# A decoder layer on one core: attention and mLSTM parts get step tables of their own, DVE makes the last weight remainders

## The reference, cut to what matters

```python
z = x @ w_in
q_a, k_a, v_a, q_idx, k_idx, w_idx, q_m, k_m, v_m, o_m, i_m, f_m = jnp.split(z, split_points, axis=-1)
y_a = _dsa_attention(...)          # score = sum_h w[t,h] relu(q_idx.k_idx); top 128 causal keys; softmax with ALiBi
qk_m = silu(causal_depthwise_conv(concat[q_m, k_m], conv_w, conv_b))
y_m = _mlstm(q_m, k_m, v_m, i_m + b_igate, f_m + b_fgate, o_m, gn_w)   # 4 heads of 128, head normalisation at the end
mix = concat([y_a, y_m]) @ w_out
x = layer_norm(alpha * x + mix);  x = layer_norm(alpha * x + hier_moe(x))
x = x + sigmoid(x @ ple_gate_w) * (p @ ple_proj_w)
```

## Time and profile before

| what | us |
|---|---|
| median of 3 runs (750.93 to 752.8) | 751.52 |
| profiled execution, its own time | 750.55 |
| its span, first to last instruction | 748.8 |
| PE busy (matmuls) | 653.2 |
| DVE busy | 338.9 |
| ACT busy | 178.6 |
| POOL busy | 208.8 |

### The profile page before, as it was taken

How to read it: one execution, slowest core, us unless ns; L and a number is a source line. 1 busy time by engine, 2 the same in 40 slices (tenths; PEclk the granted TensorE clock), 3 DMA queues, 4 the chain that set the end, 5 groups by cost and what they waited for, 6 DMA issues and landing times.

```text
span 748.8 us, 10018 instructions
## 1 busy us (share of the span) xinstructions
PE 653.2 (87%) x3782; PEld 456.1 (61%) x3782; DVE 338.9 (45%) x791; ACT 178.6 (24%) x344; POOL 208.8 (28%) x177
## 2 busy tenths in 40 slices
PE   4999649999999999899644999999999988866997
PEld 3768537787787788678532555555555544422776
DVE  3389995284265254654863211111112211148932
ACT  5264112422423313710120111111111111132230
POOL 7215400540451130450202233333333331112300
PEclk9959779999999999999875999999999999989899
DMA  6402300130130050029287688999999999957002
GB/s 242 170 1 85 140 1 0 57 141 1 56 113 1 1 224 1 2 95 397 104 347 311 232 325 296 405 416 415 413 414 415 415 416 415 414 196 285 1 35 78
DMA packets 30438, 151.21 MB, mean 202 GB/s; under 512 B 7308, under 2 KB 7564, under 8 KB 16432
## 3 DMA queue, kind: packets, MB, share of 16 engines
q1 hardware_dynamic: 23984, 142.08, 48.0%
q0 software_dynamic: 6400, 8.42, 3.1%
HBM read 148.36 MB, written 14.68 MB: 218 GB/s over the span
## 4 chain that ended last, share of the span: by engine, by line
PE 56%; DVE 12%; DMA 6%; SPq 5%; issue 3%; ACT 1%; POOL 0%; DVEq 0%; POOLq 0%; ACTq 0%
PE bank L1798 15%; PE bank L1813 8%; PE bank L1507 7%; PE bank L1509 7%; PE bank L1508 7%; SPq L422 5%; DMA raw<-in_w_exp_dram 4%; PE bank L1587 3%; PE bank L1788 2%; PE bank L1596 2%; PE bank L1608 2%; DVE res L1482 1%; DVE res L1207 1%; DVE res L1092 1%; PE bank L1637 1%
## 5 line engine op out<-in xcount | busy, mean ns | idle before, releaser
L1437 DVE COPY rows_x<-bank 128x128 f32<-128x128 f32 x40 | 11.7, 292 | 194.9 <-issue 101.3
L1507 PE MATMUL bank<-w_hi,a_hi 128*128 128x384 f32 (+1 forms) x256 | 95.7, 374 | 3.2 <-DVE w_lo L1491 1.7
L1508 PE MATMUL bank<-w_lo,a_hi 128*128 128x384 f32 (+1 forms) x256 | 94.0, 367 | 0.0
L1509 PE MATMUL bank<-w_hi,a_lo 128*128 128x384 f32 (+1 forms) x256 | 93.9, 367 | 0.0
L633 POOL DMA_INDIRECT pair_dram<-rows_x,row_put x40 | 40.5, 1013 | 166.7 <-ACT rows_x L872 166.7
L1507 PE MATMUL bank<-a_hi,w_hi 128*128 128x512 f32 (+1 forms) x176 | 70.9, 403 | 11.3 <-POOL w_lo L543 9.9
L543 POOL TENSOR_TENSOR w_lo<-raw,w_hi 128x1024 fp32r<-128x1024 f32 x19 | 45.2, 2386 | 120.8 <-ACT w_hi L680 120.7
L1798 PE MATMUL bank<-raw,rows_x 128*64 128x256 f32 x544 | 65.4, 392 | 7.0 <-DMA raw<-in_w_exp_dram 5.4
L1508 PE MATMUL bank<-a_lo,w_hi 128*128 128x512 f32 (+1 forms) x176 | 68.9, 391 | 0.0
L1509 PE MATMUL bank<-a_hi,w_lo 128*128 128x512 f32 (+1 forms) x176 | 68.7, 390 | 0.0
L1798 PEld LDWEIGHTS bank<-raw,rows_x 128*64 128x64 f32 x544 | 40.2, 141 | 36.3 <-issue 14.6
(11 more groups left out here) (238 smaller groups left out, 1016.6 us busy)
## 6 DMA issues: line engine op xcount, KB each, us to landing
raw<-in_w_exp_dram SPq DMA_DIRECT2D x42, 1024.0 KB
slots<-in_w_exp_dram SPq DMA_DIRECT2D x36, 1024.0 KB
rows_x<-in_w_exp_dram SPq DMA_DIRECT2D x12, 1024.0 KB
raw<-in_w_in_dram SPq DMA_DIRECT2D x19, 512.0 KB, 3.8
raw<-in_w_wide_dram SPq DMA_DIRECT2D x4, 1536.0 KB, 6.6
y<-in_w_exp_dram SPq DMA_DIRECT2D x6, 1024.0 KB
raw<-in_w_out_dram SPq DMA_DIRECT2D x4, 1024.0 KB, 7.8
raw<-pair_dram SPq DMA_DIRECT2D x4, 1024.0 KB, 8.7
```

The source lines that it names most:

```text
L1507: t_.matmul(o, lh, rh, start=first, stop=False)
L1508: t_.matmul(o, lh, rl, start=False, stop=False)
L1509: return t_.matmul(o, ll, rh, start=False, stop=last)
```

## The change

- Each part gets a list of step numbers, one per head. `ATTEND` gives the step of the first attention sub-step (12, 18, 24, 30), and the six follow in the six steps from there. `HEAD_QK`, `HEAD_NUM`, `BROADCAST`, `DECAY_EXP`, `CONV`, `TANH`, `CONV_END`, `HEAD_VAR` and `HEAD_OUT` do the same for the parts of an mLSTM head.
- DVE makes the remainders of pieces 11 to 18 (`split`) and of the wide weights of groups 2 and 3 (`split_wide`); POOL keeps the rest.
- `lstm_out` is in two parts, `lstm_variance` and `lstm_out`, and `convolve` too: the taps, and `convolve_end` with the product. For this the tanh has a buffer of its own for q and for k (parts of `weight` and `dist` that are free then).
- On ACT, `gates_last` of step 1 stands behind `round_piece` and `round_wide` of that step.

```diff
+        ATTEND = [12, 18, 24, 30]
+        BROADCAST, DECAY_EXP = [5, 15, 20, 28], [8, 16, 21, 29]
+        CONV, TANH, CONV_END = [[None, None], [13, 14], [19, 22], [27, 28]], [[9, 10], [15, 15], [22, 23], [28, 29]], [9, 16, 24, 30]
+        HEAD_QK, HEAD_NUM, HEAD_VAR, HEAD_OUT = [12, 17, 24, 30], [14, 19, 26, 32], [15, 20, 26, None], [16, 21, 29, None]
+        POOL_PIECES, POOL_WIDE = 11, 2
...
@@ POOL
-                if i is not None and i + RING < NPIECE:
+                if i is not None and i + RING < POOL_PIECES:
                     split(i + RING)
-                if grp is not None and j == 1:
+                if grp is not None and j == 1 and grp < POOL_WIDE:
                     split_wide(grp)
...
@@ ACT
-                if 2 * h + c >= 1:
-                    act.wait_ge(s_conv, 2 * h + c)
-                a.activation(tanh_c, conv[:, c, :], ACT.Tanh, scale=0.5).then_inc(s_ctanh, 1)
+                if h:
+                    act.wait_ge(s_conv, 2 * h)
+                    act.wait_ge(s_mdist, 6)
+                a.activation(tanh_of(h, c), conv[:, c, :], ACT.Tanh, scale=0.5).then_inc(s_ctanh, 1)
...
-                if n == step_no(0, 1):
-                    gates_last()
                 i = piece_at(n)
                 if i is not None and i + RING < NPIECE:
                     round_piece(i + RING)
                 if grp is not None and j == 1:
                     round_wide(grp)
+                if n == step_no(0, 1):
+                    gates_last()
...
@@ DVE
+            def split(i):
+                dve.wait_ge(s_wlo, i)
+                dve.wait_ge(s_whi, i + 1)
+                r = i % RAWS
+                v.tensor_tensor(ring(w_lo, i), raw[:, r * PW:(r + 1) * PW], ring(w_hi, i).bitcast(F32),
+                                ALU.subtract).then_inc(s_wlo, 1)
...
             def work(g, j):
+                now = STEPS * g + j
+                for h in range(HM):
+                    if CONV_END[h] == now:
+                        convolve_end(h, 0)
+                        convolve_end(h, 1)
+                    if 0 <= now - HEAD_QK[h] < 2:
+                        lstm_weight(h, 2 * (now - HEAD_QK[h]))
+                        lstm_weight(h, 2 * (now - HEAD_QK[h]) + 1)
+                for h in range(NG):
+                    if 0 <= now - ATTEND[h] < 6:
+                        attention(h, now - ATTEND[h])
+                if g < NG and j < TALL and POOL_PIECES <= SMALL + TALL * g + j + RING < NPIECE:
+                    split(SMALL + TALL * g + j + RING)
+                if POOL_WIDE <= g < NG and j == 1:
+                    split_wide(g)
+                for h in range(HM):
+                    if h and BROADCAST[h] == now:
+                        lstm_add(h)
+                    for c in range(2):
+                        if CONV[h][c] == now:
+                            convolve(h, c)
+                    if HEAD_VAR[h] == now:
+                        lstm_variance(h)
+                    if HEAD_OUT[h] == now:
+                        lstm_out(h)
```

More of the change, by code:

```diff
@@ L140, in hybrid_layer, with tanh_of @@
         conv = res[:, 2560:3584].rearrange("p (a t) -> p a t", a=2)
-        tanh_c = res[:, 3584:4096]
+        tanh_q = res[:, 3584:4096]
+        def tanh_of(h, c):
+            return (dist[:, :] if h else weight[:, 0:512]) if c else tanh_q
         at = [0]
@@ L574, in _ @@
                     strike_future()
[L575 removed]
+                if i is not None and i + RING < POOL_PIECES:
                     split(i + RING)
[L577 removed]
+                if grp is not None and j == 1 and grp < POOL_WIDE:
                     split_wide(grp)
[L579 to L582, removed]
+                if grp is not None:
+                    for h in range(HM):
+                        if DECAY_EXP[h] == n - SMALL:
+                            mask_decay(h)
+                        if HEAD_VAR[h] == n - SMALL:
+                            power(h)
             def split_out(q):
@@ L773, in work @@
             def work(g, j):
[L775 to L785, removed]
+                now = STEPS * g + j
+                for h in range(HM):
+                    if HEAD_NUM[h] == now:
+                        lstm_hidden(h)
+                for h in range(NG):
+                    if 0 <= now - ATTEND[h] < 6:
+                        attention(h, now - ATTEND[h])
+                for h in range(HM):
+                    if DECAY_EXP[h] == now:
+                        lstm_exp(h)
+                    for c in range(2):
+                        if TANH[h][c] == now:
+                            conv_tanh(h, c)
             def round_x(c):
@@ L1096, in convolve, with step_post, settle_post, lstm_variance @@
                     dve.wait_ge(s_mqk, 4 * h)
-                v.scalar_tensor_tensor(out=qk_m[:, c, :], in0=tanh_c, scalar=1.0, in1=conv[:, c, :], op0=ALU.add,
+                v.scalar_tensor_tensor(out=qk_m[:, c, :], in0=tanh_of(h, c), scalar=1.0, in1=conv[:, c, :], op0=ALU.add,
                                        op1=ALU.mult).then_inc(s_conv, 1)
[L1100 to L1110, removed]
+            POST, POST_VAR = 17, 12
+            post = [0]
+            def step_post(ins):
+                post[0] += 1
+                ins.then_inc(s_post, 1)
+            def settle_post():
+                dve.wait_ge(s_post, post[0])
+            def lstm_variance(h):
+                assert post[0] == POST * h
+                step, settle = step_post, settle_post
                 dve.wait_ge(s_hid, 2 * (h + 1))
@@ L1132, in lstm_out @@
                 v.tensor_scalar(den, mean_var[:, :, 1:2].squeeze(2), EPS, None, ALU.add).then_inc(s_var, 1)
+            def lstm_out(h):
+                assert post[0] == POST * h + POST_VAR
+                step, settle = step_post, settle_post
+                hid = hidden[:, :, 0:P]
                 dve.wait_ge(s_pow, h + 1)
@@ L1153, in attention @@
                     attn_out(g)
-            def work(g, j):
[L1156 to L1170, removed]
+            def split(i):
[4 more added lines that the diff above has]
+                                ALU.subtract).then_inc(s_wlo, 1)
@@ L1182, in _ @@
                     if i == 7:
-                        lstm_out(NG - 1)
+                        lstm_variance(HM - 1)
+                        lstm_out(HM - 1)
                     dve.wait_ge(s_yhi, i + 1)
@@ L1650, in work @@
             def work(g, j):
[L1651 to L1662, removed]
+                now = STEPS * g + j
+                for h in range(HM):
+                    if HEAD_NUM[h] == now:
+                        lstm_num(h)
+                    if BROADCAST[h] == now:
+                        lstm_broadcast(h)
+                    if 0 <= now - HEAD_QK[h] < 2:
+                        lstm_qk(h, 2 * (now - HEAD_QK[h]))
+                        lstm_qk(h, 2 * (now - HEAD_QK[h]) + 1)
+                for h in range(NG):
+                    if 0 <= now - ATTEND[h] < 6:
+                        attention(h, now - ATTEND[h])
             for n in range(SMALL):
```

14 lines of the change are left out of this document (13 added, 1 removed).

## The result

The changed kernel takes 740.62 us (738.57 to 742.01, 6 runs) against 753.48 for the kernel before (750.93 to 755.23, 6 runs on the same chips): ratio 0.983, interval 0.9803 to 0.9857, 12.9 us faster. The forecast was 20.6 us faster. A second set of runs gave 740.0 and 0.9824 (0.9796 to 0.9853). The profiled executions, 750.55 and 740.59, are 10.0 us apart.

A forecast was written before the change was run, and what follows sets the result against it. PE was taken as saturated except where its in-order queue waits twice on DVE's `top_keys`. Terms -23.0 + 1.5 - 1.7 + 2.6 = -20.6 us from the median 751.52 gave 731 us, range 727 to 736.

The forecast's parts named there:

- rival A: DVE becomes the bound of steps 13 to 30, with extras at their upper bound: about 740 us; chance 0.19.
- part 1: Work up to step 13: PE's idle front gap is filled, 23.0 us sooner, after 0.65 lost by moving `gates_last`.
- part 2: Stall at step 13, from DVE's late mask and piece 13's load, rounding and split: 1.5 us lost, bounds 0 and 5.
- The front gap filled: PE's waits of 6.86 and 10.97 us during DVE's `top_keys` filled with projections: 23.0 us sooner if nothing stalls.
- The mask held by POOL's wide split: End of `top_keys`: DVE's mask waits for POOL's wide split until 116.1, instead of being reached at 113.9.
- piece 13's round trip: Loaded only after piece 11's split: 3.8 load, 1.05 rounding, 1.15 split, ready at 126.7, with PE's step 13 ending at 127.1.
- DVE's extras: DVE's added work beside attention, steps 13 to 31: +2.6 us, bounds 0 and 12; 0.8 lost at step 15, 1.3 at 20.
- part 3: DVE beside attention, steps 13 to 31: three `lstm_qk` waits go, -1.7 us, and extras cost +2.6 us.
- The waits that go, -1.7: Three of the `lstm_qk` waits of 0.56 us, one place per group, disappear: 1.7 us gained.
- B: PE cannot run ahead as steps 8 to 11 stick; only 9.3 us comes back, about 742 us; chance 0.08.
- C: Every DVE split waits its whole round trip, 6.0 us each, up to 48 us for eight pieces: 773; chance 0.04.
- D: The change moves nothing, as a later stage such as the expert stage takes the gain back: 751 us; chance 0.03.

The follow-up runs named there:

- experiment 1: Changed kernel with `gates_last` put back ahead of `round_piece` and `round_wide` in step 1 on ACT; 733.57 us, ratio 0.9711.
- experiment 2: Kernel before with only `gates_last` moved behind `round_piece` and `round_wide` in step 1; 761.32 us, ratio 1.0081.
- experiment 6: Changed kernel with DVE's gate rows called after the first round of `top_keys` (r == 0); 731.6 us, ratio 0.9705.
- the repeat: experiment 6 run again unedited, as yardstick beside experiment 9; 731.26 us, ratio 0.9703.
- experiment 8: experiment 1 with the norm undivided (`HEAD_OUT` equal to `HEAD_VAR`); 746.55 us, ratio 0.991.
- experiment 3: Changed kernel with gate rows called after the second round of `top_keys` (r == 1) instead of the third; 738.21 us, ratio 0.9759.
- experiment 4: Changed kernel with POOL making every remainder again, none on DVE; 745.56 us, ratio 0.9864.
- experiment 7: Changed kernel with `gates_last` first in step 1 and POOL making every remainder; 739.93 us, ratio 0.9836.
- experiment 9: experiment 6 with gate columns after round index 6 of `top_keys` instead of 7; 740.13 us, ratio 0.9818.
- experiment 11: experiment 9 with head 0's second convolution after round index 12 instead of 13; median 740.62 us, ratio 0.9823, two of six runs near 733.

## Why the prediction was wrong

The forecast's own range ended at 736 us and the one with rival A at 740; 740.62 lies outside both, by 4.6 and 0.6 us. The gain fell short by 7.7 of 20.6 us, and one step is enough to explain it.

- *The step that failed* is in part 1: "PE loses about 0.65 (bounds 0 and 2.1, the whole delay of the Exp)" by the move of `gates_last`. I followed the move on ACT and from there to PE and to POOL, and even noted that POOL's wide remainder now starts at 68.4. I did not ask what DVE does at that time, though in part 2 I had the lock between the two, with its price. DVE was in L989 and L990. The move costs 6.4 to 8.4 us with the tables and 6.5 without (experiments 1 and 2); in the trace 6.63 us of waiting, and step 3 at half clock for most of it (77.26 to 85.4, some 2.5 us more than a narrow step), while what it gave was 3.2 us less of waiting for the wide remainder, with a slower step behind.
- *The front gap filled*: right. With the lock out of the way (experiment 6) the output projection starts at 299.80, against the forecast's 299.5, and the kernel is 22 us faster where 20.6 was forecast. That close a match is partly luck. The first `lstm_qk` stands 3.1 us behind the forecast (123.42 against 120.35), for the wait of 1.97 us on the gate columns and the slower clock behind it, which the forecast had ruled out; the stretch from there to the output projection took 2.8 us less than I had (176.4 against 179.2). In the repeat the two points are 121.54 and 297.83.
- *The mask held by POOL's wide split, and piece 13's round trip* (part 2): right as mechanisms. L1039 takes 4.13 us instead of 0.90, DVE waits 3.97 us on ACT's rounding, ACT 8.43 on the DMA. PE loses 0.51 us behind step 13 and 0.46 ahead of step 12; I had 1.5.

```profile
122.24 4.13 DVE L1039 TENSOR_SCALAR raw<-raw 128x256 f32<-128x256 f32 x3
...
135.54 1.23 DVE L1186 TENSOR_TENSOR w_lo<-raw,w_hi 128x1024 fp32r<-128x1024 f32 x1 [3.97 <-ACT w_hi L697]
```

- *DVE's extras* (part 3): too dear. I charged 0.8 at step 16 and 1.3 at step 21; PE shows neither. At step 21 DVE comes to its mask at 209.83, 1.14 us behind PE's first `qk` (208.69). In step 9 before the change that was 0.95 us (140.06, 139.11), so DVE is 0.2 us late and not 1.3. Sub-step 3 takes 212.54 - 208.69 = 3.85 us, what it took there. The room is about 1 us larger than I counted, since PE's `qk` comes before DVE is needed again. Beyond that room it gets dear at once: experiment 8 put about 3.6 us more into the same places and lost 13.

```profile
207.99 1.93 DVE L1086 TENSOR_SCALAR res<-bank,a_col 128x512 f32<-128x512 f32 x4
209.83 0.55 DVE L1053 CUSTOM_DVE_ANT_0 raw<-bank,pa 128x384 f32<-128x384 f32 x1
```

- *The waits that go, -1.7* (part 3): counted once too often. Of the three in the earlier trace rows, 12.0 us in all, the longest (11.0) was already in part 1, so two were left, worth 1.0 us. The changed kernel still has one (0.49 us at 280.05).
- *What was hidden by another error*: in this profile about 3 us went to a clock dip (below) that I had not foreseen, about as much as parts 2 and 3 together were too dear (179.7 us from the first `lstm_qk` to the output projection, 179.2 forecast, 176.4 in experiment 6, which has no such dip there).
- Rival A (DVE the bound, about 740) names the measured time, but not its cause: no gap in most steps, one at step 3. Rivals B, C and D did not occur in the changed kernel.

Put together from the runs, against about 754: tables and parts -13.7, DVE's splits -6.4 to -7.5, the move of `gates_last` +6.4 to +8.4; measured in all -12.9 and -13.7.

The lock is the rule of the Trainium skill, page "SBUF — State Buffer", section "Who interferes with whom", and its other half is now visible too: a `tensor_scalar` (L990, L1039) is held like the two-input operations. By the page that form can use the shared port in its fast mode. The runs show the wait; of the mode they show only that it would fit: unheld, L990 takes 0.41 us where the two-input L989 of the same size takes 0.68. I wrote at the start of this text that the engines meet only through semaphores; these two also meet here.

## What to carry to other kernels

When an operation is moved on one engine, look at what every other engine does at the time at which its followers now start: here ACT's reordering let POOL's two splits start 3.2 to 3.6 us earlier, into the last two of six DVE instructions on 4 partitions. Long POOL operations that read SBUF beside a DVE that is on the path are best counted as windows in which DVE may not start a two-input or `tensor_scalar` operation; the price is the rest of the window, not a share of it, and half a microsecond decides whether it is paid. DVE's `max` and `match_replace` were not held: three MAX8 take 1.47 us from 119.16, inside POOL's wide split, and 1.46 from 98.69 with POOL quiet; MATCH_REPLACE8 on 512 columns takes 0.68 and 0.66. Such schedules should be judged on several runs, since one of them fell on either side from run to run.

## What the runs showed that I had not expected

A very small instruction can be the dearest: L990 works on 4x512 and took 6.87 us in five profiles of four kernels (the changed one twice, experiments 2, 3 and 4), because POOL's wide split had just begun.

TensorE's clock went to its lower level (0.50 of 2.4 GHz, that is 1.2) with PE marked busy throughout. In the changed kernel, in windows of 3 us:

```profile
153.00:156.00 3.00, 3.00 (x13) 1.68 (x11) 0.77 (x2) 0.61 (x3) 0.00 (x0) 1.00 0.00 0
156.00:159.00 3.00, 3.00 (x13) 1.68 (x13) 1.48 (x5) 0.71 (x2) 0.00 (x0) 0.81 0.00 0
159.00:162.00 3.00, 3.00 (x13) 2.71 (x13) 1.46 (x8) 1.85 (x4) 0.00 (x0) 0.50 0.00 0
162.00:165.00 3.00, 3.00 (x9) 2.36 (x8) 2.90 (x12) 0.00 (x0) 0.94 (x1) 0.55 0.00 0
```

PE had done a broadcast and sub-step 3 of attention behind four wide steps that each had attention work beside them. Steps 15 and 16 took about 3 us longer for it: 160.47 - 155.40 for the sub-step instead of 3.86, and 167.97 - 160.47 = 7.5 instead of 5.55 for the projection. The same kernel's second profile has short dips there and at step 20, and one at 308 to 316; experiments 1 and 6 have none at 156 but one of about 7 us behind the last sub-steps (300 to 307). The kernel before, with attention work beside two wide steps of four, has none between 120 and 328 us. Other profiles have dips near 200 us (experiments 3, 7 and 8) or 265 to 275 us (4, 8, 9 and 11). What sets them off stays open; it was not tried apart. Since they come and go between profiles of one kernel, a difference of 3 us between two single profiles says little.
